# A decoder step with a mixture of experts: modulation weights in column pieces, projections accumulated piece by piece, one weight transfer per expert for gate and up

## The reference

```python
sh_m, sc_m, g_m, sh_f, sc_f, g_f = split(silu(c) @ ada_w + ada_b, 6)      # c: 9 sequences, ada_w: 1024 x 6144
xn = rmsnorm(x, norm_mix_g) * (1 + sc_m) + sh_m
xa, ga, pu, pv = split(xn @ w_in, 4)                                      # 512 columns each
xc = causal_conv(xa)                                                      # width 4
r, i = sigmoid(xc @ wr + br), sigmoid(xc @ wi + bi)                       # blocks of 64
a = exp(-8 * r * softplus(-lam)); h = scan(a * h + sqrt(1 - a*a) * i * xc)
ya = h * gelu(ga)
yb = gelu(pu) * spatial_gate(rmsnorm(gelu(pv)))                           # causal 128 x 128 per head
x = x + g_m * (group_rmsnorm(concat(ya, yb)) @ w_out)
xn = rmsnorm(x, norm_ffn_g) * (1 + sc_f) + sh_f
gates = top 8 of 64 experts from sigmoid(xn @ router_w), normalised, times 2.5
x = x + g_f * (sum_e gates_e * swiglu_e(xn) + swiglu_shared(xn))          # each 1024 -> 256 -> 1024
y = rmsnorm(x, final_norm_g)
```

## Time and profile before

| | |
|---|---|
| median of 3 runs | 802.32 us (798.81 to 806.03) |
| profiled execution | 803.89 us, span 802.2 us, mean granted TensorE clock 0.962 |
| TensorE matmul busy | 706.3 us (88%) |
| VectorE, ScalarE, GpSimd busy | 325.1, 228.4, 301.4 us |
| DMA queues | SP's 252.35 MB, 79.3% of the 16 engines' span; GpSimd's 26.07 MB, 13.5% |
| chain that ended last | TensorE 63%, DMA 28%, VectorE 5% |

### The profile page before, as it was taken

The page is one execution under the profiler, slowest core; times in us unless marked ns, Lnnn a source line. Parts: engine busy times, 40 slices in busy tenths (PEclk is TensorE's granted clock), DMA queues, the critical chain, the costliest instruction groups (busy, mean ns, idle before and its releaser), DMA issues.

```text
span 802.2 us, 14713 instructions
## 1 busy us (share of the span) xinstructions
PE 706.3 (88%) x4965; PEld 396.7 (49%) x4966; DVE 325.1 (41%) x601; ACT 228.4 (28%) x392; POOL 301.4 (38%) x317
## 2 busy tenths in 40 slices
PE   3699999999999999999999999999889978998830
PEld 1277556445565446554555555454455533544510
DVE  3115475476533544334322432434322433243217
ACT  4202622023223322233222322323222332232212
POOL 0321011021305553356444553636446454454230
PEclk9799999999899999999999999999999999999985
DMA  8999979719489999899999999999999999999944
GB/s 327 363 297 323 337 260 327 294 58 394 151 325 387 390 410 409 304 386 382 395 384 392 393 391 400 388 408 401 405 413 401 400 401 409 399 402 402 382 93 136
DMA packets 74818, 279.14 MB, mean 348 GB/s; under 512 B 18997, under 2 KB 22193, under 8 KB 49040
## 3 DMA queue, kind: packets, MB, share of 16 engines
q1 hardware_dynamic: 51240, 252.35, 79.3%
q0 software_dynamic: 23424, 26.07, 13.5%
q10 hardware_dynamic: 104, 0.08, 0.0%
HBM read 272.54 MB, written 26.30 MB: 373 GB/s over the span
## 4 chain that ended last, share of the span: by engine, by line
PE 63%; DMA 28%; DVE 5%; issue 2%; SPq 1%; ACT 1%; POOL 0%; POOLq 0%; DVEq 0%; ACTq 0%
PE bank L1119 25%; DMA gu<-in_exp_w_up 24%; PE bank L1155 11%; PE bank L864 5%; PE bank L855 5%; PE bank L982 3%; DMA gu<-in_ada_w 3%; PE bank L1097 2%; PE bank L830 2%; PE bank L867 1%; PE bank L1211 1%; PE bank L1136 1%; PE bank L1066 1%; PE bank L1093 1%; PE bank L968 1%
## 5 line engine op out<-in xcount | busy, mean ns | idle before, releaser
L1119 PE MATMUL bank<-gu,et 128*64 128x256 f32 x2496 | 287.8, 385 | 27.5 <-DMA gu<-in_exp_w_up 22.1
L1119 PEld LDWEIGHTS bank<-gu,et 128*64 128x64 f32 x2496 | 184.5, 139 | 148.5 <-issue 73.4
L538 POOL DMA_INDIRECT acc_rows<-et,idx x64 | 104.6, 1635 | 241.7 <-DVE et L1644 143.6
L1155 PE MATMUL bank<-dn,et 128*64 128x512 f32 x632 | 149.7, 602 | 11.8 <-issue 9.5
L1637 DVE COPY et<-bank 128x256 f32<-128x256 f32 x64 | 27.2, 424 | 253.5 <-PE bank L1136 253.5
L726 ACT ACTIVATE et<-bank 64x512 f32<-64x512 f32 x64 | 37.9, 592 | 259.0 <-PE bank L1119 259.0
L1155 PEld LDWEIGHTS bank<-dn,et 128*64 128x64 f32 x632 | 40.4, 136 | 78.7 <-issue 78.7
L736 ACT ACTIVATE et<-bank,mb 128x512 f32<-128x512 f32 x64 | 44.0, 688 | 122.6 <-PE bank L1155 99.3
L1644 DVE TENSOR_SCALAR et<-bank,mb 128x512 f32<-128x512 f32 x64 | 48.0, 751 | 70.0 <-PE bank L1155 55.7
L1630 DVE TENSOR_TENSOR et<-et 64x512 f32<-64x512 f32 x64 | 67.9, 1060 | 0.4 <-ACT et L727 0.4
L548 POOL DMA_DIRECT2D small<-halfc x49 | 56.3, 1148 | 0.0
(11 more groups left out here) (290 smaller groups left out, 633.7 us busy)
## 6 DMA issues: line engine op xcount, KB each, us to landing
dn<-in_exp_w_down SPq DMA_DIRECT2D x64, 1024.0 KB, 25.2
gu<-in_exp_w_gate SPq DMA_DIRECT2D x63, 1024.0 KB, 23.6
gu<-in_exp_w_up SPq DMA_DIRECT2D x63, 1024.0 KB, 26.4
gu<-in_ada_w SPq DMA_DIRECT2D x12, 2048.0 KB, 15.0
gu<-in_w_in SPq DMA_DIRECT2D x3, 2048.0 KB, 19.1
gu<-in_w_out SPq DMA_DIRECT2D x2, 2048.0 KB, 16.4
acc_rows<-late SPq DMA_DIRECT2D x2, 1280.0 KB, 14.7
gu<-in_w_in SPq DMA_DIRECT2D x2, 1024.0 KB, 15.4
```

What stands on the lines that cost most here:

```text
L538: pool.indirect_dma_start(acc_rows[u % 2], bass.IndirectOffsetOnAxis(ap=idx[:, u, 0:1], axis=0), yo[:, u % 2, 0, :], None, bounds_check=2 ...
L1119: mm = pe.matmul(bank[u % 2][64 * c:64 * c + 64, b * FE:(b + 1) * FE], xt[:, b, k % 4, k // 4, :], w[c][:, k * FE:(k + 1) * FE], start=(k ...
L1155: mm = pe.matmul(bank[5 + b][64 * c:64 * c + 64, :], hT[:, b, j, :], dn[:, dslot(u), j * D + c * HALF:j * D + (c + 1) * HALF], start=(j == ...
```

## The change

Modulation and projection weights, `w_out` and the shared and routed gate and up weights come in new arrays, laid out before the launch (`laid_out`) so that each load is one run of 16 KB per partition (8 KB for the small projection pieces). `mix` piece m now holds all rows of the 512 columns that give shift and scale of two rows k of `xT`; a projection piece `lru_in_w` holds the xa and ga columns of the same two rows. So TensorE can turn the coefficients of two rows (`mix_turn`), VectorE and ScalarE scale these rows, and TensorE adds their share to the four xa channels and to the first ga channel (`channel_step`; this one in bank 1) while the next pieces load. The other ga channels follow. v's first tile comes next, then piece 4, v's other tiles, the gates with piece 5 between, and u's first tile ahead of pieces 8 and 9. ScalarE has v's gelus and squares ahead of the gates' sigmoids. `PIECES` and `used` are replaced by `HOME` (slot and turn of each piece) and a written out order of loads with waits. Gate and up of an expert are one transfer (`exp_gu`), except for the fifth, whose halves still go to two places. The core of the diff; removed lines of TensorE, VectorE and SyncE are left out where the listing above has them:

```diff
-        eu = io["exp_w_up"][0].rearrange("e (p k) f -> e p (k f)", k=KT)
+        HOME = {("mix", 0): (0, 1), ("mix", 2): (0, 2), ("in", 3): (0, 3), ("ada", 8): (0, 4), ("out", 0): (0, 5),
+                ("mix", 1): (1, 1), ("mix", 3): (1, 2), ("in", 2): (1, 3), ("out", 1): (1, 4),
+                ("ada", 4): (2, 2), ("ada", 6): (2, 3), ("ada", 9): (2, 4), ("ada", 11): (2, 5),
...
+        E_SLOT = 3
+        lru_w = [gu[2 + m][:, :, :].rearrange("p k n -> p (k n)").rearrange("p (k n) -> p k n", k=4) for m in range(2)]
+        lru_in = [ld_piece[2], s["ld_in0"], ld_piece[3], s["gn_fin"]]
...
-        PRJ = ([("xa", c) for c in range(CT)] + [("ga", c) for c in range(CT)] + [("r", c) for c in range(CT)]
-               + [("i", c) for c in range(CT)] + [("v", t) for t in range(3)] + [("u", t) for t in range(3)])
+        PRJ = ([("xa", c) for c in range(CT)] + [("ga", c) for c in range(CT)] + [("v", t) for t in range(3)]
+               + [("r", c) for c in range(CT)] + [("i", c) for c in range(CT)] + [("u", t) for t in range(3)])
...
         def prj_bank(n):
-            return bank[4 + prj_no[n] % 4]
+            return bank[1] if n == ("ga", 0) else bank[4 + prj_no[n] % 4]
...
+            load("mix", 0, io["mix_w"][0])
+            load_lru(0)
+            load("mix", 1, io["mix_w"][1])
+            load_lru(1)
...
+            for r0, src in rows:
+                sync.dma_start(chrow[r0:r0 + src.shape[0], :], src).then_inc(s["ld_ch"], 16)
+            sync.wait_ge(s["mix_used"], 1)
+            load("mix", 2, io["mix_w"][2])
+            load_lru(2)
+            sync.wait_ge(s["mix_used"], 2)
+            load("mix", 3, io["mix_w"][3])
+            load_lru(3)
+            sync.wait_ge(s["mix_used"], 3)
+            load("in", 3, io["sgu_in_w"][1])
...
+            sync.dma_start(wnat, io["sgu_w"][0].rearrange("g p q -> p g q")).then_inc(s["ld_sgu"], 16)
+            sync.wait_ge(s["mix_used"], 4)
+            load("in", 2, io["sgu_in_w"][0])
+            sync.wait_ge(s["prj_ready"], prj_no[("ga", CT - 1)] + 1)
+            load("ada", 4, io["ada_rest"][0])
+            load("ada", 5, io["ada_rest"][1])
...
+            sync.wait_ge(s["mod_ready"], 1)
+            load("ada", 6, io["ada_rest"][2])
+            sync.wait_ge(s["prj_ready"], prj_no[("v", 2)] + 1)
+            load("ada", 8, io["ada_rest"][4])
+            sync.wait_ge(s["mod_ready"], 2)
+            load("ada", 7, io["ada_rest"][3])
+            sync.wait_ge(s["mod_ready"], 3)
+            load("ada", 9, io["ada_rest"][5])
+            sync.wait_ge(s["mod_ready"], 4)
+            load("ada", 10, io["ada_rest"][6])
+            sync.wait_ge(s["mod_ready"], 5)
+            load("out", 0, io["out_w"][0])
+            sync.wait_ge(s["mod_ready"], 6)
+            load("ada", 11, io["ada_rest"][7])
+            sync.wait_ge(s["prj_ready"], prj_no[("u", 2)] + 1)
+            load("out", 1, io["out_w"][1])
+            sync.wait_ge(s["mod_ready"], 8)
+            sync.dma_start(guf[SH_SLOT], io["shared_in_w"]).then_inc(ld_shared_gu, 16)
...
-                sync.dma_start(guf[sl][:, 0:KT * FE], eg[e]).then_inc(ld_gu[sl], 16)
-                sync.dma_start(guf[sl][:, KT * FE:2 * KT * FE], eu[e]).then_inc(ld_gu[sl], 16)
+                sync.dma_start(guf[sl], egu[e]).then_inc(ld_gu[sl], 16)
...
@@ -638,6 +647,22 @@
                                b[:, NPR:T].rearrange("p (b j) -> p b j", b=NB), ACT.Copy).then_inc(s["prj_evac"], 1)
             for c in range(CT):
...
+
+            def gelu(kind, dst):
+
+                for t, (t0, n) in enumerate(TILES):
+                    b = prj(kind, t)
+                    if t < 2:
+                        act.activation(dst[:, t, :], b[:, :], ACT.Gelu_apprx_tanh).then_inc(s["prj_evac"], 1)
+                    else:
+                        act.activation(dst[0:64, 2, 0:FE], b[0:64, 0:FE], ACT.Gelu_apprx_tanh).then_inc(s["gelu_half"], 1)
+                        act.activation(dst[0:64, 2, FE:W], b[64:P, 0:FE], ACT.Gelu_apprx_tanh).then_inc(s["prj_evac"], 1)
+            gelu("v", vv)
+            act.wait_ge(s["gelu_half"], 1)
+            for t, (t0, n) in enumerate(TILES):
+                act.wait_ge(s["prj_evac"], prj_no[("v", t)] + 1)
...
+            def channel_step(m):
+                pe.wait_ge(lru_in[m], 16)
+                pe.wait_ge(s["mix_s"], 2 * m + 2)
+                pe.wait_ge(s["mix_v"], m + 1)
+                pe.wait_ge(s["mix_a"], m + 1)
+                for c in range(CT):
+                    channels(("xa", c), c * P, (2 * m, 2 * m + 1))
+                channels(("ga", 0), W, (2 * m, 2 * m + 1))
 
...
+            def mix(m):
+                w = piece("mix", m)
+                if m:
+                    pe.wait_ge(s["mod_evac"], m)
+                for k in range(KT):
+                    for g in range(4):
+                        mm = pe.matmul(bank[0][32 * g:32 * g + 32, 0:P], cT[:, k, :], w[:, k, g * P:(g + 1) * P],
+                                       start=(k == 0), stop=(k == KT - 1))
                 mm.then_inc(s["mix_used"], 1)
+
+            def mix_turn(m):
+                pe.wait_ge(s["mod_evac"], m + 1)
+                if m:
+                    pe.wait_ge(s["mix_coef"], 2 * m)
+                else:
+                    pe.wait_ge(s["tp_evac"], TP["x21"] + 1)
+                pe.transpose(bank[2][:, 0:P], mods[:, m, :], ident[:, :]).then_inc(s["modT_ready"], 1)
 
             mix(0)
             turn("x", "xn_done", 0)
             turn("x", "xn_done", 1)
             turn("x", "xn_done", 2)
+            mix_turn(0)
+            for m in range(4):
+                if m < 3:
+                    mix(m + 1)
+                if m == 3:
...
+                channel_step(m)
+                if m < 3:
+                    mix_turn(m + 1)
+            for c in range(1, CT):
+                prj_wait("ga", c)
+                channels(("ga", c), W + c * P, range(KT))
...
+
+            tokens("v", 3, 0)
             ada(4)
+            tokens("v", 3, 1)
+            tokens("v", 3, 2)
             pe.wait_ge(s["ld_rg"], 64)
             pe.wait_ge(s["conv_done"], 1)
+            gates("r", wr)
+            ada(5)
+            gates("i", wi)
...
+            ada(6)
+            ada(7)
+            tokens("u", 2, 0)
...
+            for m in range(4):
+                k = 2 * m
+                dve.wait_ge(s["mix_used"], m + 1)
+                dve.tensor_tensor(mods[:, m, :], bank[0][:, 0:P], adab[:, m, :], ALU.add).then_inc(s["mod_evac"], 1)
+                dve.wait_ge(s["modT_ready"], m + 1)
+                modT = bank[2][:, 0:P].rearrange("p (a h c) -> p a h c", a=2, h=2)
+                dve.scalar_tensor_tensor(mixA[:, k:k + 2, :], modT[:, 1, :, 0:NSEQ], 1.0,
+                                         gnT[:, k:k + 2].rearrange("p (k o) -> p k o", o=1).to_broadcast([P, 2, NSEQ]),
                                          ALU.add, ALU.mult).then_inc(s["mix_coef"], 1)
+                dve.tensor_copy(mixB[:, k:k + 2, :], modT[:, 0, :, 0:NSEQ]).then_inc(s["mix_coef"], 1)
+                dve.wait_ge(s["mix_coef"], 2 * m + 2)
+                dve.wait_ge(s["tp_evac"], TP["x21"] + 1)
+                xs = xTs[:, k:k + 2]
+                dve.tensor_tensor(xs, xs, over_t(mixA, k), ALU.mult).then_inc(s["mix_s"], 1)
                 dve.tensor_scalar(xT[:, k, 0:NPR], xT[:, k, 0:NPR], mixA[:, k, 0:1], mixB[:, k, 0:1], ALU.mult, ALU.add).then_inc(s["mix_v"], 1)
+                dve.wait_ge(s["mix_s"], 2 * m + 1)
+                dve.tensor_tensor(xs, xs, over_t(mixB, k), ALU.add).then_inc(s["mix_s"], 1)
...
+def laid_out(np, inputs):
...
+    return {
+        "exp_gu": np.concatenate(exp, axis=2),
+        "mix_w": ada[:, :, 0:2 * D].reshape(P, KT, 2, 4, 2 * P).transpose(3, 0, 1, 2, 4).reshape(4, P, 4 * D),
+        "ada_rest": ada[:, :, 2 * D:].reshape(P, KT, 8, W).transpose(2, 0, 1, 3).reshape(8, P, 4 * D),
+        "lru_in_w": win[:, :, 0:D].reshape(4, 2, P, D).transpose(0, 2, 1, 3).reshape(4, P, 2 * D),
```

More of the change, by code:

```diff
@@ L229, in build @@
-        ed = io["exp_w_down"][0].rearrange("e (p j) n -> e p (j n)", j=2)
[L232 to L251, removed]
+        HOME = {("mix", 0): (0, 1), ("mix", 2): (0, 2), ("in", 3): (0, 3), ("ada", 8): (0, 4), ("out", 0): (0, 5),
+                ("mix", 1): (1, 1), ("mix", 3): (1, 2), ("in", 2): (1, 3), ("out", 1): (1, 4),
+                ("ada", 4): (2, 2), ("ada", 6): (2, 3), ("ada", 9): (2, 4), ("ada", 11): (2, 5),
+                ("ada", 5): (3, 2), ("ada", 7): (3, 3), ("ada", 10): (3, 4)}
@@ L339, in _, with load, load_lru @@
-            sync.wait_ge(*used(SH_NO - SLOTS))
-            for c, name in enumerate(("shared_w_gate", "shared_w_up")):
-                sync.dma_start(gu[SH_SLOT][:, :, c * FE:(c + 1) * FE],
-                               io[name][0].rearrange("(p k) f -> p k f", k=KT)).then_inc(ld_shared_gu, 16)
+            def load(kind, j, src):
+                sl = HOME[(kind, j)][0]
```

(38 more changed lines are left out.)

204 lines of the change are left out of this document (74 added, 130 removed).

## The result

The changed kernel takes **826.95 us** (median of 4 runs, 821.38 to 833.08), the kernel before on the same chip 801.89 (798.81 to 806.03): ratio 1.032, 95% interval 1.026 to 1.039. It is slower, where 795 was forecast with 784 to 820. The profiled execution took 823.02, its span is 821.2.

The account below looks back on a forecast made before the run. TensorE was taken to bound the prologue from 37 to 134 us, the weight transfers the expert loop, with TensorE close to full; 803.9 less 4 (prologue) and 4.5 (packets) gave 795.4, predicted as 795, range 784 to 820.

Parts of the forecast that it names:

- the forecast: Whole kernel: prologue and packet gains both come, 795 us, within 791 to 798; chance 0.38.
- the first rival: Expert loop: GpSimd's gathers and scatters queue behind larger packets, holding the output buffer; slower, 815 to 840 us, chance 0.2.
- upper end of 14.5: Expert loop: highest landing time in us expected for copy and scatter, against 12.5 expected; costs 20 to 50 us.
- The threshold: Output buffer in the loop: waiting for the scatter two experts back decides from about 13 us of landing on.
- The rows named against it: Expert loop: VectorE's waits for scatters are few, 7 with 11.2 us in all, which spoke against slower landings costing time.
- Packets, 4.5 us (0 to 8.8): Expert loop: eight fewer packets per engine and expert, at most 0.018 us each, gain 4.5 us over 60 experts.
- The prologue, 4 us (0 to 9): Before the loop: early accumulation gains 8.7 us, v ahead of the gates gives back 4.8; 4 us left.
- the recurrence at the sums: Prologue: the recurrence's last square ends at 112.4 us, so TensorE, at the group sums at 110, waits 2.4 us.
- one piece late at 97 us: Prologue: a modulation piece could land late at 73 or 97 us, helping to give back the prologue's gain.
- cold clock: Prologue: TensorE at the low clock for one or two steps; one warm-up costs 2.2 us, two 4.4.
- the second rival: Prologue: it gives back everything, leaving only the packets' part or not even this; 797 to 803 us, chance 0.25.
- A shift of the prologue passes through: Prologue to loop: TensorE loses only 22.1 us to weight waits, so a prologue shift reaches the kernel's end.

Follow-up runs that it names:

- e4: The kernel before with only gate and up of an expert in one transfer with 16 KB packets; 833.41 us, ratio 1.039.
- e9: The changed kernel with gathers issued four experts ahead in place of three, 16 KB packets and two output buffers kept; 823.45 us, ratio 1.028.
- e1: The changed kernel with gate and up again in two transfers of 1,024 KB, 8 KB packets; 798.73 us, ratio 0.999.
- e2: The changed kernel with gate and up still one transfer of 2,048 KB, but cut into 8 KB packets; 799.32 us, ratio 1.000.
- e13: The changed kernel, 16 KB packets, with gathers four experts ahead, four output buffers and arrays, and 16 index-list slots; 812.70 us, ratio 1.015.
- e14: The changed kernel with gathers four experts ahead, four output buffers and arrays, 16 index-list slots, and 8 KB packets; 804.44 us, ratio 1.0045.
- e7: The kernel before (old prologue) with only 24 of the 64 experts computed; 467.47 us.
- e12: The changed kernel with 8 KB packets and u's first tile put between modulation pieces 6 and 7; 797.30 us, ratio 0.9936 against the kernel before.
- e8: The changed kernel (new prologue), gate and up in one transfer with 8 KB packets, only 24 of the 64 experts computed; 466.79 us.
- e6: The changed kernel with gate and up in one transfer cut into packets of 4 KB; 804.17 us, ratio 1.0035.
- e3: The changed kernel with gate and up in two transfers by halves of the partitions, each 64 packets of 16 KB; 1,170.95 us.

## Why the prediction was wrong

**The step that failed** is the choice between the forecast and the first rival. The rival was right in kind, sign and place: GpSimd's gathers and scatters queue behind larger packets, and the output buffer's eviction waits for them. I gave it 0.2, and nothing in the sum, because I put the landing at 12.5 us, under the 13 from which it decides; for that I counted only two thirds of the further 8 KB. With 16 KB the medians are 13.6 (gathers) and 14.3 (tiny copies) in e4, and the landings in the changed kernel's chain, the late ones by nature, are 12.4 to 16.1: near the upper end of 14.5, which counts all 8 KB. Its price, 815 to 840, holds 827. The threshold itself was about right: in e9, where the output buffer alone holds the loop, the copies' median is 13.4. (By its own rows the threshold sum gives 8.2 and 9.2 us per expert, not 8.4 and 9.4; that moves no choice.) The rows named against it ("few such waits now") say little of a wait that has a threshold: 7 waits of up to 2.8 us can as well mean that the landing was already next to it.

Beside this stands the rule of the Trainium skill ("DMA: Bandwidth & Descriptors", section "Queues, rings and completion order") that an engine drains a packet of several descriptors from one ring before it turns to the next. The runs agree: beside 8 KB pieces, in two transfers or in one, GpSimd's gathers land in 8.9 and 9.6 us (e1, e2), beside 16 KB pieces in 13.6 (e4).

**What I didn't see** is that the late landing acts in three places one behind the other: output buffer, gather (whose issue stands on GpSimd behind the scatter), index list. Removing the first alone gave 832.5 (ratio 1.039), the second alone 823.5 (1.028), both 817.3 (1.018), all three 812.7 (1.015). About 18 of the 26 us are shown to be these waits. The 8 left are in part late landings as well: the early experts' output still waits for a scatter two back (a landing of 14.4 us in e13's chain at 240 us, of 11.9 in e14's), and with a median of 22.3 and a longest of 31.2 us the gathers are late again even with four experts of lead. How much of the 8 us is theirs is open.

**Packets, 4.5 us (0 to 8.8).** Mis-sized: none of it shows. Rates at 8 and 16 KB are alike where the stream is full (398 to 407 GB/s before and 401 to 407 after, in the full stretches from 450 us on that have a DMA share of 1.02 or more), and 4 KB cost 0.003 us a packet, against my upper bound of 0.018 and the half of it that I took. The slower piece in the 2 KB stretch, with rows far apart, is the likely source of the difference; no run shows it. The 78% at 1 MB that the Trainium skill ("DMA: Bandwidth & Descriptors", section "Bandwidth") gives, for transfers that GpSimd issues, isn't seen in SyncE's full queue: two transfers of 1,024 KB (e1) are as fast as one of 2,048 (e2), 402 GB/s each.

**The prologue, 4 us (0 to 9).** In the trace of after the times are those of the forecast: ga 65.2 (66), piece 4 at 73.2 (73), sums at 112.2 (112.4), pieces 10 and 11 at 129.5 (130.0). What TensorE waits for is not, so part of this was luck: 3.07 us for the load of piece 7, where I had one product "waiting a little", and nothing for the recurrence at the sums, where I had 2.4 us (its last square ends at 111.3). Wrong as a mean: I had "one piece late at 97 us" and "cold clock" in the second rival, as two things; the gap is in all twelve profiles, and the cold clock follows in nine. Over all profiles of the two orders the gain at pieces 10 and 11 is then near 1 us (ends of 131.6 and 133.0 on average). The "before" of my sum was also a single trace: e7 shows 132.2 for its 133.9, e4 132.9, and for its 214.5 at the shared expert they show 211.2 and 210.3. That end depends on the clock ahead of it, in before and, below it, after:

```profile
200.00:210.00 10.00, 10.00 (x31) 6.30 (x32) 8.80 (x21) 2.85 (x10) 3.34 (x3) 0.66 0.34 95
```

```profile
200.00:210.00 10.00, 8.83 (x57) 4.78 (x57) 4.69 (x9) 2.74 (x7) 7.13 (x8) 0.97 0.44 121
```

The gap ahead of piece 7 is the slot's: that piece is requested when piece 5's product ends, at 90.1, and is there 9.5 us later.

**A shift of the prologue passes through.** At 8 KB most of it does: the shared expert ends at 214.5, 212.7, 208.9 and 207.7 us in before, e2, e1 and e12, and the spans are 802.2, 801.0, 798.9 and 796.6. At 16 KB it can't be told: the ratios with the old and the new prologue, 1.039 (e4) and 1.032, have intervals that overlap.

## What to carry to other kernels

Before packets of a stream are enlarged, look at what else uses the DMA engines: here the landing of small transfers on another queue grew from 9 to 14 us when the stream's pieces went from 8 to 16 KB, for no gain in rate. A wait that is short and rare can be just under its threshold; ask how much longer its cause may take, and what stands behind it when it is removed. A short gap in front of TensorE can cost more than its length (in e8 3.3 us, and 2.8 more at the low clock behind it), and a single trace doesn't show how often.

## What the runs showed of the hardware

- Pieces of 4 and 8 KB per partition moved 397 and 402 GB/s from 450 to 740 us (e6, e2); pieces of 16 KB moved 401 to 407 in full stretches of 50 us (after). Gathers landed in 9.6 us (8 KB, e2) and 13.6 (16 KB, e4).
- Transfers over 64 of 128 partitions with 16 KB pieces moved 241 GB/s (e3).
- With 16 KB pieces, a longer queue of gathers and scatters landed later, 22.3 us median in e13, at the same number per time.
- A wait of 3 us for a load was followed by a granted clock of 0.73 to 0.87 in the stretch from 100 to 112 us in nine of twelve profiles of the same instruction order, and by 1.00 in the other three.
